# Last expert of a mixture-of-experts trunk summed in token rows, on top of turned blocks of the residual stream

## The reference

```python
    logits = (x @ router).astype(jnp.float32)
    top_val, top_idx = lax.top_k(logits, TOP_K)
    ...
    for e in range(N_EXPERTS):
        y = y + gates[..., e:e + 1].astype(x.dtype) * swiglu(x, wg[e], wu[e], wd[e])
    ...
    return rms_norm(h, norm_final)[:, N_META:]
```

## Time and profile before

| | us |
|---|---|
| median of 3 runs | 2157.16 |
| lowest and highest run | 2152.53 and 2158.5 |
| span of the profiled execution | 2157.6 |
| busy in it: PE, DVE, ACT | 2098.1, 1466.4, 1233.0 |

### The profile page before, as it was taken

One profiled execution on the slowest core, in us unless ns is written; L12 is line 12 of the kernel. 1 busy time (PEld: TensorE's weight loads), 2 busy tenths in 40 slices (PEclk: granted clock), 3 DMA queues, 4 the chain that ended last, 5 costly groups with the idle time before them and its releaser, 6 DMA issues.

```text
span 2157.6 us, 36168 instructions
## 1 busy us (share of the span) xinstructions
PE 2098.1 (97%) x15316; PEld 1821.0 (84%) x15316; DVE 1466.4 (68%) x1329; ACT 1233.0 (57%) x1148; POOL 22.1 (1%) x24
## 2 busy tenths in 40 slices
PE   9999999999999999999999999999999999999997
PEld 7877789999999797788997788888888888888886
DVE  5633438454443773334848889898988888889895
ACT  4454445343333455445446777777777777777674
POOL 0000100000000000010000000000000000000000
PEclk9999999999999999999999999999999999999998
DMA  6333105344443232210537989899898989889893
GB/s 239 126 78 121 57 3 197 155 157 185 167 157 139 78 117 98 79 42 14 223 118 293 359 331 377 345 359 368 335 376 322 382 331 373 351 351 372 330 371 116
DMA packets 73839, 484.89 MB, mean 225 GB/s; under 512 B 12424, under 2 KB 13576, under 8 KB 15992
## 3 DMA queue, kind: packets, MB, share of 16 engines
q1 hardware_dynamic: 72440, 479.43, 57.5%
q10 hardware_dynamic: 1280, 3.70, 0.5%
HBM read 481.36 MB, written 1.74 MB: 224 GB/s over the span
## 4 chain that ended last, share of the span: by engine, by line
PE 91%; DVE 5%; ACT 2%; issue 1%; DMA 1%; SPq 0%; DVEq 0%; ACTq 0%
PE PS L530 23%; PE PS L532 23%; PE PS L531 23%; PE PS L943 5%; PE PS L809 2%; PE PS L827 2%; DVE area L1743 2%; PE PS L1195 2%; DVE WL L1743 1%; PE PS L1202 1%; PE PS L688 1%; PE PS L851 1%; ACT WH L1657 1%; DMA ring<-in_experts 1%; PE PS L602 1%
## 5 line engine op out<-in xcount | busy, mean ns | idle before, releaser
L1743 DVE TENSOR_TENSOR WL<-ring,WH 128x2048 fp32r<-128x2048 f32 x410 | 934.3, 2290 | 251.4 <-ACT WH L1320 142.3
L1657 ACT ACTIVATE WH<-ring 128x2048 fp32r<-128x2048 f32 x336 | 642.8, 1916 | 170.7 <-PE PS L532 138.4
L530 PE MATMUL PS<-WH,XGH 128*128 128x512 f32 x896 | 354.6, 396 | 3.0 <-DVE XGL L1743 2.4
L532 PE MATMUL PS<-WL,XGH 128*128 128x512 f32 x896 | 350.2, 391 | 0.0
L531 PE MATMUL PS<-WH,XGL 128*128 128x512 f32 x896 | 349.6, 390 | 0.0
L1320 ACT ACTIVATE WH<-ring 128x2048 fp32r<-128x2048 f32 x74 | 141.4, 1911 | 119.8 <-PE PS L532 119.7
L532 PE MATMUL PS<-XL,WH 128*128 128x272 f32 (+1 forms) x704 | 202.6, 288 | 0.0
L530 PEld LDWEIGHTS PS<-WH,XGH 128*128 128x128 f32 x896 | 168.7, 188 | 38.1 <-DVE XGL L1743 2.6
L532 PEld LDWEIGHTS PS<-WL,XGH 128*128 128x128 f32 x896 | 168.4, 188 | 35.9
L531 PEld LDWEIGHTS PS<-WH,XGL 128*128 128x128 f32 x896 | 168.9, 188 | 33.6
L530 PE MATMUL PS<-WH,HTH 128*128 128x512 f32 x448 | 176.8, 395 | 1.2 <-DVE WL L1743 0.7
(11 more groups left out here) (339 smaller groups left out, 3563.1 us busy)
## 6 DMA issues: line engine op xcount, KB each, us to landing
ring<-in_experts SPq DMA_DIRECT2D x336, 1024.0 KB, 6.7
ring<-in_weights SPq DMA_DIRECT2D x114, 1024.0 KB, 6.8
ring<-in_weights SPq DMA_DIRECT2D x4, 576.0 KB, 6.3
ring<-in_weights SPq DMA_DIRECT2D x4, 512.0 KB, 4.4
cst<-in_consts ACTq DMA_DIRECT2D x1, 1731.0 KB, 9.0
area<-in_x ACTq DMA_DIRECT2D x2, 512.0 KB, 4.7
out<-area SPq DMA_DIRECT2D x4, 256.0 KB, 2.2
bias_line<-lin SPq DMA_DIRECT2D x1, 672.0 KB
```

What stands on the lines that cost most here:

```text
L530: pe.matmul(o, lh, rh, start=first, stop=False, skip_group_check=True)
L532: return pe.matmul(o, lh, rl, start=False, stop=last, skip_group_check=True)
L1657: act.activation(WH[(BASE + j + 1) % 3][:, :], ring[b][:, 2048 * (j % 2):2048 * (j % 2) + 2048], ACT.Copy).then_inc(S("w_hi"), 1)
L1743: tt = lambda o, a_, b_, op: dve.tensor_tensor(o, a_, b_, op)
```

## The change

- The last expert's body no longer gathers for a ninth expert: no `gather` on PE, no copies of its result (L1673 on ACT, the subtraction on DVE), no selection matrix for it on DVE.
- The last expert is no longer scattered to features x tokens and added to `hT`. Behind the branch PE instead turns 16 blocks of `hT` (128x128, 2 token blocks x 8 feature tiles) into PSUM banks 2, 3, 6, 7 and leaves the accumulation open; then 8 matmuls with `SELT` as the stationary operand and `YEH` or `YEL` as the moving one (512 columns) add the last expert's rows to them.
- `YEH` and `YEL` of the last expert are made in two halves of 512 columns each, with a semaphore for each half (`y_hi`, `y_lo`).
- ACT squares the finished rows out of PSUM, 128x1024 for each token block, with the sum over the row as a by-product (`accum_out`). `column_sums` goes.
- The gain is no longer applied to `hT`. A copy of it in each partition (`gain_row`, 4 KB each, 512 KB in all) is loaded by SP behind the last chunk of layer 1's weights and ahead of the experts' loads. All four output pieces are made by DVE, row scale and gain in one instruction.
- ACT takes one root of a spare value in the last expert's body, ahead of `YEH`.
- In the second pass the scatter of the first pass's last expert stands at the front of `first_gather`.

```diff
+            sp.dma_start(gain_row, bass.AP(tensor=gain.tensor, offset=0, ap=[[0, P], [1, D]])).then_inc(S("gain_in"), 16)
             for_all_experts(sp, expert_loads)
...
                     if (kind, f, half) == ("d", FG - 2, 0):
                         turn_hidden(n, FG - 1)
-
-                        gather(n + run + 2)
-
-                pe.wait_ge(S("e_xgl"), n + run + 2)
+                        if not last:
+                            gather(n + 2)
                 if not last:
+                    pe.wait_ge(S("e_xgl"), n + 2)
                     half_products(n + 1, 0)
-
-                pe.wait_ge(S("e_stc"), n * 2 + 2)
+                    pe.wait_ge(S("e_stc"), n * 2 + (2 - run))
+                    scatter()
...
+            for_all_experts(pe, expert_products, first_gather, last_rows)
+            pe.wait_ge(S("e_chain"), (NE - 1) * 5)
+            pe.wait_ge(S("e_stc"), (NE - 1) * 2 + 1)
+            for t in range(2):
+                for q in range(2):
                     for k in range(4):
-                        ins = pe.transpose(PS[:, 1 + 2 * t + q, k * P:(k + 1) * P], xn[:, 4 * q + k, 1 + META + t * P:1 + META + (t + 1) * P],
-                                           C("ident"))
-                ins.then_inc(S("fin_pe"), 1)
+                        pe.matmul(PS[:, rows_bank(t, q), k * P:(k + 1) * P], hT[:, 4 * q + k, META + t * P:META + (t + 1) * P], C("ident"),
+                                  start=(k == 0), stop=False, is_transpose=True, skip_group_check=True)
+            for sem, y in (("y_hi", YEH), ("y_lo", YEL)):
+                for q in range(2):
+                    pe.wait_ge(S(sem), q + 1)
+                    for t in range(2):
+                        ins = pe.matmul(PS[:, rows_bank(t, q), :], SELT[:, t * P:(t + 1) * P], y[:, 512 * q:512 * q + 512],
+                                        start=False, stop=(y is YEL), skip_group_check=True)
+                        if y is YEL and q:
+                            ins.then_inc(S("fin_rows"), 1)
...
+                if last:
+                    act.activation(small[:, 50:51], small[:, 49:50], ACT.Sqrt)
+                    act.wait_ge(S("w_used"), used(n, "d", FG - 1))
+                    act.wait_ge(S("e_stc"), n * 2 + (1 - run))
+                    for q in range(2):
+                        act.activation(YEH[:, 512 * q:512 * q + 512], PS[:, 4 + q, :], ACT.Copy, scale=MR[:, 187:188]).then_inc(S("y_hi"), 1)
+                    return
...
+            for t in range(2):
+                act.wait_ge(S("fin_rows"), t + 1)
+                act.activation(hnT[:, t, :].rearrange("p (a b) -> p a b", a=2), PS[:, rows_bank(t, 0):rows_bank(t, 0) + 2, :], ACT.Square,
+                               accum_out=MR[:, 188 + t:189 + t]).then_inc(S("fin_act"), 1)
             act.wait_ge(S("fin_dve"), 1)
...
             act.activation(MR[:, 184:186], MR[:, 184:186], ACT.Sqrt).then_inc(S("fin_act"), 1)
...
+            for_all_experts(dve, expert_hidden, first_select)
+            dve.wait_ge(S("fin_act"), 2)
+            dve.tensor_scalar(MR[:, 184:186], MR[:, 188:190], 1.0 / D, EPS, ALU.mult, ALU.add).then_inc(S("fin_dve"), 1)
             dve.wait_ge(S("fin_act"), 3)
             dve.reciprocal(MR[:, 184:186], MR[:, 184:186]).then_inc(S("fin_dve"), 1)
...
+            for t in range(2):
+                for q in range(2):
+                    cols = slice(512 * q, 512 * q + 512)
+                    dve.scalar_tensor_tensor(ostage[:, t, cols], PS[:, rows_bank(t, q), :], MR[:, 184 + t:185 + t], gain_row[:, cols],
+                                             ALU.mult, ALU.mult).then_inc(S("out_copied"), 1)
```

More of the change, by code:

```diff
@@ L122, with build_trunk @@
 NWEIGHT = _at
-def build_trunk(nc, x, meta, weights, experts, router, w2, a2, g2, vw1, vw2, rel_bias, consts, params, out):
+def build_trunk(nc, x, meta, weights, experts, router, w2, a2, g2, vw1, vw2, rel_bias, gain, consts, params, out):
     chunks = CHUNKS
@@ L290, in build_trunk, with rows_bank @@
         ostage = area2[:, 0:2 * D].rearrange("p (a n) -> p a n", a=2)
+        gain_row = VF[:, :, :].rearrange("p a t -> p (a t)")[:, 0:D]
+        def rows_bank(t, q):
+            return (2, 3, 6, 7)[2 * t + q]
         LAST = (3, 5, 5, 5, 5)
@@ L506, in _ @@
                     sp.dma_start(buf[:, half * 4 * width:(half + 1) * 4 * width], src).then_inc(S(f"landed{i % RING}"), 16)
+            sp.dma_start(gain_row, bass.AP(tensor=gain.tensor, offset=0, ap=[[0, P], [1, D]])).then_inc(S("gain_in"), 16)
             for_all_experts(sp, expert_loads)
-            for q in range(2):
-                for t in range(2):
-                    sp.wait_ge(S("out_copied1" if t else "out_copied0"), q + 1)
+            for t in range(2):
+                for q in range(2):
+                    sp.wait_ge(S("out_copied"), 2 * t + q + 1)
                     sp.dma_start(out[0, t * P:(t + 1) * P, 512 * q:512 * q + 512], ostage[:, t, 512 * q:512 * q + 512]).then_inc(S("out_stored"), 16)
@@ L656, in router_part @@
                     ins.then_inc(S("q_turn"), 1)
[L658 to L666, removed]
             for l in range(DEPTH):
@@ L1242, in expert_products, with scatter @@
                         turn_hidden(n, FG - 1)
[L1244 to L1246 removed]
+                        if not last:
+                            gather(n + 2)
                 if not last:
+                    pe.wait_ge(S("e_xgl"), n + 2)
                     half_products(n + 1, 0)
[L1250 removed]
+                    pe.wait_ge(S("e_stc"), n * 2 + (2 - run))
+                    scatter()
+            def scatter():
                 for k in range(KT):
@@ L1258, in first_gather, with last_rows @@
             def first_gather(pe, run):
-                gather(run * (NE + 1) + 1)
-                pe.wait_ge(S("e_xgl"), run * (NE + 1) + 1)
-                half_products(run * NE, 0)
[L1264 to L1268, removed]
-                    for k in range(4):
-                        ins = pe.transpose(PS[:, 1 + 2 * t + q, k * P:(k + 1) * P], xn[:, 4 * q + k, 1 + META + t * P:1 + META + (t + 1) * P],
-                                           C("ident"))
-                ins.then_inc(S("fin_pe"), 1)
+                if run:
+                    pe.wait_ge(S("y_lo"), 2 * run)
+                    scatter()
+                gather(run * NE + 1)
+                pe.wait_ge(S("e_xgl"), run * NE + 1)
+                half_products(run * NE, 0)
+            def last_rows(pe):
+                pe.wait_ge(S("e_chain"), (PASSES * NE - 1) * 5)
+                pe.wait_ge(S("y_lo"), 2 * PASSES)
+            for_all_experts(pe, expert_products, first_gather, last_rows)
[3 more added lines that the diff above has]
+                for q in range(2):
+                    for k in range(4):
+                        pe.matmul(PS[:, rows_bank(t, q), k * P:(k + 1) * P], hT[:, 4 * q + k, META + t * P:META + (t + 1) * P], C("ident"),
[8 more added lines that the diff above has]
+                            ins.then_inc(S("fin_rows"), 1)
         @block.scalar
@@ L1692, in expert_highs @@
                         do(f)
[L1693 to L1696, removed]
+                if last:
[5 more added lines that the diff above has]
+                    return
+                gathered_high(act, n + 2)
+                expert_high(n + 1, 0)
+                expert_high(n + 1, 1)
                 act.wait_ge(S("w_used"), used(n, "d", FG - 1))
-                act.wait_ge(S("e_stc"), n * 2 + 1)
+                act.wait_ge(S("e_stc"), n * 2 + (1 - run))
                 act.activation(YEH[:, :].rearrange("p (a b) -> p a b", a=2), PS[:, 4:6, :], ACT.Copy, scale=MR[:, 187:188]).then_inc(S("e_y"), 1)
-                if not last:
-                    for j in range(2, AHEAD):
-                        expert_high(n + 1, j)
+                for j in range(2, AHEAD):
+                    expert_high(n + 1, j)
             def first_highs(act, run):
-                for j in range(1 if isinstance(run, int) else 0, 3):
+                for j in range(0 if run else 1, 3):
                     expert_high(run * NE, j)
-                gathered_high(act, run * (NE + 1) + 1)
+                gathered_high(act, run * NE + 1)
                 for j in range(3, AHEAD):
@@ L2232, in select_tokens @@
                 def select_tokens(f):
+                    if last:
+                        link_e(2, dve.memset(small[:, 51:52], 0.0))
+                        return
                     link_e(2, dve.tensor_copy(MR[:, 162:164], slots[:, :, bass.ds(e + 1, 1)]))
-                    dve.wait_ge(S("e_xg"), n + run + 1)
+                    dve.wait_ge(S("e_xg"), n + 1)
                     select_next(S("e_sel"))
@@ L2269, in expert_hidden @@
                         do(f)
[L2270 to L2273, removed]
-                rows_low()
[L2275 to L2281, removed]
+                if last:
+                    for q in range(2):
```

(26 more changed lines are left out.)

4 lines of the change are left out of this document (2 added, 2 removed).

## The result

The changed kernel takes 2143.18 us (median of 10 runs, 2139.71 to 2153.8) against 2158.1 us (median of 10, 2152.53 to 2162.7). The ratio is 0.9937 with a 95% interval of 0.9923 to 0.9952, so it is faster by 0.6%.

What follows compares the result with a forecast made beforehand. Engines waiting in turn take 23.6 us behind the last product. Saving 3.57 us there from the gather and 10.4 behind that product takes 14.0 off 2157.6: 2143.6, stated as 2143.5 against the median, range 2139.5 to 2149.

Steps and rivals of the forecast that it cites:

- Gather: Last expert: dropping its gather saves all 3.57 us, since the last half's low part has 0.7 us to spare.
- PE's branch: Behind the last product: 0.9 us from flag to branch, then 3.36, mostly hidden; PE stands still 1.05 us.
- Turns and rows: PE after its branch: 16 turns at full clock, 1.76 us, then eight row matmuls at 0.228; block 0 done at 2135.1.
- Squares: Final norm: two squares of 1.06 us, row sums 0.1 each, to 2137.4; mean, root and reciprocal 0.63, to 2138.05.
- Output: Four output pieces on DVE take 2.8 us, to 2140.85; then 2.78 us to the span's end, 2143.6.
- Sum: Whole change: 3.57 us from the gather and 10.4 behind the last product, together 14.0 of 2157.6, giving 2143.6.
- Rival A: Final norm on ACT: the root's table is loaded again behind the squares, adding 1.1 us, 2144.6; chance 0.2.
- Rival B: Behind a branch on PE or ACT: a second instruction-stream stop, up to 2.4 us, 2145.9 or 2145.5; chance 0.12.
- C: Last expert: the gather's 3.57 us are given back because the last halves wait for low parts, 2147; chance 0.05.
- D: Whole change: no measurable change, needing several costs at once; even 9.4 us together leave 2153.0; chance 0.05.
- E: Ahead of the experts' loads: a slow gain load makes their weights late, 2171 if it took 100 us; chance 0.02.

Runs made afterwards that it cites:

- the repeat: The changed kernel unaltered, measured again on the chip used for the end by token block: 2144.28 us (5 runs), ratio 0.9933 to the kernel before.
- the eight loads: The changed kernel with the gain's load made eight times, each waiting for the one before, ahead of the experts' loads: span 2140.4 us.
- the run by token block: The changed kernel with row matmuls, root and output taken by token block: 2143.18 us with turns ahead of PE's branch, 2142.29 us with them behind.

## Why the prediction was right

Point by point, each against its own step:

- **Gather.** 3.57 us forecast, 3.57 measured, and the same in the run that changed nothing else. The spare of the last low part was enough.
- **PE's branch.** 1.05 us of PE standing still forecast, 1.26 measured (1.3 in the repeat, 1.65 with a branch of 3.9 us in another run). The flag was read 3.3 us ahead of the last product's end; I had it at 2.75 to 3.25. For DVE I had allowed a stop of up to 3.36 us hidden behind its branch; the run with the scatter kept shows one of 2.9, and the 0.19 us ahead of the add in the kernel before is its end and no hand-over. ACT's is no longer than 3.4.
- **Turns and rows.** First square 4.65 us behind the last product by the sum, 4.85 measured. The turns took 1.7 us from start to the first row matmul (2129.41 to 2131.1), as forecast. The full clock that both need did hold, but the reason given for it, that it had held over 7 us in the kernel before, isn't a safe one: in two small variants of that kernel it fell 2.6 and 4.0 us behind the last product, and at the lower level the step would have cost 2.6 us more, as in the run with 40 unexecuted matmuls. That it held is in part luck.
- **Squares.** 1.02 us each, and the row sum is an instruction of its own, ACTIVATION_READ_ACCUMULATOR, of 0.2 us, half hidden: together 2.13, where I had 2.3. Mean, root and reciprocal 0.73 us (0.63 forecast).
- **Output.** 2.73 us for the four pieces (2.8 forecast), and 2.5 from the last of them to the end of the span (2.78). The last store took 0.33 us to issue, not 0.39; the rest of the difference lies between its issue and the end of the span (2.15 us instead of 2.37), and its cause is open.
- **Sum.** Tail 13.15 forecast, 12.9 measured. The errors of single terms, 0.2 to 0.3 us, have both signs.
- **Rival A** did not come: no table load stands behind the branch, one (1.28 us) stands ahead of the early root, under the last products. So where both paths that meet end in the same table, none was put in, and by-block placement as the Trainium skill has it (ScalarE activation tables: per-element evaluation and per-set limits, "Table sets in the compiler and the runtime") didn't force one. The price given was right: 1.1 us in the run without the early root. That run shows no drain: the load starts at 2136.86, takes 1.28 us, and the whole way from the squares to the reciprocal is 1.54, less than the 2.66 us a switch of the Trainium skill (ScalarE: Activation LUTs, "What ACT_TABLE_LOAD costs").
- **Rival B** did not come either, but it was under-priced. It is real in both kernels and hangs on the place of code alone. I gave 2.4 us for it; in the changed kernel it comes with 5.8, as the clock falls during the stop. The Trainium skill (Runtime: NRT & Kernel Launch, "Instruction fetch mechanics") speaks of blocks of 256 instructions. My count of PE's instructions took a float32 matmul as four and any other as two, and used that figure. No run here shows the block's length by itself, but both trials that moved the landing point, by 20 and by 160 instructions, came out as this count had said before they ran.
- **Rivals C, D and E** are ruled out by the run without the gather, by the tail of 12.9 us, and by the eight loads, in this order.

What the forecast didn't have: the last product ended at 2128.15 in this trace, 2.3 us ahead of the sum. Nothing shows this to be an effect of the change. It lies ahead of the last expert and differs from run to run: 2128.15 and 2132.43 in two profiles of the changed kernel, and, with 3.57 us for the gather taken off where there is one, 2127.19, 2128.08 and 2130.45 in the three profiles of the kernel before and its variants. In the two profiles of the changed kernel the first expert's gather starts 8.3 us apart already, at 1130.26 and 1138.53. What sets it was not looked into. That the predicted time met the median to 0.3 us is therefore luck to the extent of some us; that the gain is 14 us of known parts is not.

How the 14.3 us divide, by these runs: 3.6 the gather, 5.7 the new norm, 5.0 the accumulation in rows. Inside the last two stand 2.6 us of a stop of PE that the change lost by where its code lies, about 1.4 us of PE work that now is done before the clock falls, and 0.6 us of DVE's stop behind its branch. So of the 14.3 us, 2.6 are no merit of the change.

## What to carry to other kernels

At the end of a program, where engines wait for each other in turn, count hand-overs and visits to PE, not operations: one visit less, with the row sum taken on ACT, gave about 3 us beside the 2.6 of the stop. Keep a branch's cost under queued work, but don't queue so much that PE's sequencer is held up ahead of it: here 4 turns did no harm and 16 did. And compare two kernels with a branch in them only after moving the landing point on purpose: code that is never run cost 5.8 us here.

## What the runs showed of the hardware

- A taken branch on PE took 3.4 to 4.0 us in every profile here, and in three of them (the kernel before, the one without the gather, the changed one with 40 unexecuted matmuls) PE stopped again after three or four matmuls, for 1.75 to 2.6 us. On ACT and DVE the branch's own row is 54 and 63 ns. Behind it DVE's next instruction came after 2.9 us twice, with its data ready. In the run by token block ACT's first square followed its rows at once 3.4 us after its branch, so that any stop there is no longer.
- PE read the flag 3.2 to 3.4 us ahead of the last product's end with no turn or 4 turns between the products and the branch, and 0.6 us ahead of it with 16.
- The granted clock fell from the 2.4 to the 1.2 GHz level 2.6 to 4.0 us behind the last product in five profiles, in all of which PE had stood for 2 us or more by then, and 7.5 to 10.5 us behind it in the other eight. Six of these eight are profiles in which PE stood 1.0 to 1.7 us ahead of its last work; in the other two, the kernel before and the one with the scatter kept (8.2 and 8.0 us), it had stood over 2 us all the same. So a long stand doesn't always bring the fall, and when it comes is not settled here. At the lower level turns took 0.21 to 0.23 us each instead of 0.11, and a 512-column row matmul 0.43 instead of 0.23 (in the run with 40 unexecuted matmuls): PE's idle time can cost twice, in itself and in the work behind it.
